# The second mixer's output product in three parts, with projections and taps as filler in its attention

## What is computed

```python
n = rms_norm(h, mix_norm[l])
p = n @ w_in[l]
u_conv, q, k, v, q_mem = jnp.split(p, splits, axis=-1)
y_conv = conv_module(u_conv, ...)            # below
q = apply_rope(rms_norm(q, swa_q_norm[l]), cos, sin)     # 6 heads of 64
k = apply_rope(rms_norm(k, swa_k_norm[l]), cos, sin)     # 2 heads
y_swa = sliding_window_attention(q, k, v, sinks)         # window 128
mkv = rms_norm(mem, mem_norm[l]) @ w_mem_kv[l]           # 256 memory tokens
mk, mv = jnp.split(mkv, 2, axis=-1)
mk, qm = rms_norm(mk, mem_k_norm[l]), rms_norm(q_mem, mem_q_norm[l])
y_mem = memory_attention(qm, mk, mv)                     # 4 heads
y = jnp.concatenate([y_conv, y_swa, y_mem], axis=-1)     # 384 + 384 + 256
h = h + y @ w_out[l]

def conv_module(u, w_dw, b_dw, ln_g, ln_b):
    a, gate = jnp.split(u, 2, axis=-1)                   # 384 channels each
    y = a * jax.nn.sigmoid(gate)
    y = causal_depthwise_conv(y, w_dw, 31 taps) + b_dw
    return jax.nn.silu(layer_norm(y, ln_g, ln_b))
```

## Time and profile before

| | us |
|---|---|
| median of three runs | 2496.94 (2491.99 to 2501.63) |
| the profiled execution | 2497.42 |
| its span | 2495.6 |
| second mixer, first pass, from the last sum of the norm ahead to the last output matmul | 160.3 |
| of it before the first score product / attention / output tiles | 64.6 / 65.9 / 29.8 |
| second mixer, second pass | 164.3 |
| PE busy over the span | 2334.3 |
| VectorE / ScalarE busy over the span | 1543.6 / 1087.3 |

### The profile page before, as it was taken

How to read it: one execution, slowest core, us unless ns; L and a number is a source line. 1 busy time by engine, 2 the same in 40 slices (tenths; PEclk the granted TensorE clock), 3 DMA queues, 4 the chain that set the end, 5 groups by cost and what they waited for, 6 DMA issues and landing times. The chain is left out here.

```text
span 2495.6 us, 37523 instructions
## 1 busy us (share of the span) xinstructions
PE 2334.3 (94%) x13974; PEld 1990.5 (80%) x13974; DVE 1543.6 (62%) x2861; ACT 1087.3 (44%) x1896; POOL 59.4 (2%) x73
## 2 busy tenths in 40 slices
PE   6999989999999999989999999979999999978998
PEld 3656777989976587788998999747997999747997
DVE  4786606677633572376776766763766766763765
ACT  2323334555533234254555554343554554344544
POOL 0000001200000000020000000000000000000000
PEclk8989999999999999999999999979999999979999
DMA  7755222444545423224544554203553455203552
GB/s 310 266 191 188 102 102 78 171 157 181 188 167 221 178 102 127 77 107 174 200 179 154 198 196 177 102 26 139 192 195 131 177 190 188 102 26 125 197 183 92
DMA packets 37540, 390.17 MB, mean 156 GB/s; under 512 B 4416, under 2 KB 5056, under 8 KB 5952
## 3 DMA queue, kind: packets, MB, share of 16 engines
q1 hardware_dynamic: 37440, 388.87, 42.1%
HBM read 387.80 MB, written 1.05 MB: 156 GB/s over the span
## 5 line engine op out<-in xcount | busy, mean ns | idle before, releaser
L1272 PE MATMUL bank<-h,ring 128*128 128x256 f32 x2048 | 476.9, 388 | 9.7 <-ACT h L1063 8.1
L1272 PEld LDWEIGHTS bank<-h,ring 128*128 128x128 f32 x2048 | 388.6, 193 | 100.7 <-issue 29.1
L701 DVE TENSOR_TENSOR ffn_w_lo<-ring,ffn_w_hi 128x2048 fp32r<-128x2048 f32 x126 | 288.8, 2292 | 165.5 <-ACT ffn_w_hi L650 165.4
L571 PE MATMUL bank<-ffn_hh,ffn_w_hi 128*128 128x512 f32 x1408 | 363.9, 399 | 13.3 <-DVE ffn_hh L831 11.0
L571 PEld LDWEIGHTS bank<-ffn_hh,ffn_w_hi 128*128 128x128 f32 x1408 | 257.6, 192 | 67.4 <-issue 10.2
L623 PE MATMUL bank<-ffn_g_hi,ffn_w_hi 128*128 128x256 f32 x1056 | 299.3, 283 | 6.1 <-DVE ffn_g_lo L746 6.1
L623 PE MATMUL bank<-ffn_g_lo,ffn_w_hi 128*128 128x256 f32 x1056 | 298.8, 283 | 0.0
L623 PE MATMUL bank<-ffn_g_hi,ffn_w_lo 128*128 128x256 f32 x1056 | 298.8, 283 | 0.0
L650 ACT ACTIVATE ffn_w_hi<-ring 128x2048 fp32r<-128x2048 f32 x126 | 239.9, 1904 | 0.8
L623 PEld LDWEIGHTS bank<-ffn_g_hi,ffn_w_hi 128*128 128x128 f32 x1056 | 202.7, 192 | 7.4 <-issue 7.4
L623 PEld LDWEIGHTS bank<-ffn_g_hi,ffn_w_lo 128*128 128x128 f32 x1056 | 202.7, 192 | 0.0
(11 more groups left out here) (277 smaller groups left out, 3289.5 us busy)
## 6 DMA issues: line engine op xcount, KB each, us to landing
ring<-w_in SPq DMA_DIRECT2D x244, 1536.0 KB, 6.4
x<-x_in SPq DMA_DIRECT2D x1, 1024.0 KB, 15.2
mem<-mem_in SPq DMA_DIRECT2D x1, 1024.0 KB, 4.9
y_out<-x SPq DMA_DIRECT2D x4, 256.0 KB, 2.5
con<-con_in SPq DMA_DIRECT2D x1, 801.0 KB, 6.9
par<-par_in SPq DMA_DIRECT2D x2, 302.0 KB, 15.6
work<-pos_in SPq DMA_DIRECT2D x2, 128.0 KB, 6.0
par<-par_in SPq DMA_DIRECT2D x2, 76.0 KB, 4.7
```

Source lines behind the costliest of these rows:

```text
L571: pe.matmul(up_out(j, half, False), w_hi[:, j % 2, c0:c0 + P], hh[:, k, :, :], start=k == 0, stop=False)
L701: dve.tensor_tensor(w_lo[:, j % 2, UP], ring[:, (base + j) % RING, UP], w_hi[:, j % 2, UP], ALU.subtract).then_inc(S(tag + "_up_lo"), 1)
L1272: m = pe.matmul(ps[0:m_rows, 0:T], tile(t0 + k, base)[:, 0:m_rows], rhs, start=k == 0, stop=k == len(src) - 1 and kind != "uk")
```

## The change

The list is written out anew, and the parts of it move as follows.

- The memory's norm is split. Its sum on PE (now in bank 6) stands after `q` 1; its Ln, Exp and VectorE's products stand in step 0 of the attention, after `qm` 1 (`("mem", "scale", 0)`).
- The head of the list has `ca` 2, `cg` 2, `cg` 0, `ca` 0, `cg` 1, `k`, `q`, `v`, `qm` 0. `mk` 0 and 1, `ca` 1, `mv` 0 and 1 and six of eight first output parts lie in the attention.
- The taps of a block are summed in two buffers, even taps in `cvo` and odd ones in `cvo_odd`; a tap waits for the last but one, and one add joins the two. The loops over registers are gone. The blocks run one after the other, block 1 in pieces of 6, 6, 6, 6 and 5 taps in steps 4 to 8.
- The output product is made in three parts, `oa` (window attention, three matmuls a tile), `ob` (memory, two) and `oc` (convolution, three). All eight tiles accumulate at once, two to a bank in banks 0 to 3. VectorE adds them to x in pairs after every second `oc`.
- The layer norm uses bank 4, in steps 10 and 11 and after them. The log-and-exp table set is asked for after the last Sigmoid (`cg` 1), the Silu set after the layer norm's Exp.
- The weights are laid out in the new order; their count is the same.

```diff
+IN_ATTENTION = [
+    proj("qm", 1) + [("mem", "scale", 0)],
+    [("sq", "qm", 0)] + proj("mk", 0, 1) + taps(0, 2),
...
+    out_part("oa", 0, 1) + taps(1, 4),
...
+          + out_part("oa", 6, 7) + [("ln", "", 2)] + out_part("ob", *range(8)) + out_part("oc", *range(8)))
+OUT_K = {"oa": (3, 4, 5), "ob": (6, 7), "oc": (0, 1, 2)}
...
-                with dve.Fori(k0, k1) as k:
-                    for i, b_ in enumerate(blocks):
-                        dve.wait_ge(sem, k * n + (i + 1 - n))
-                        dve.scalar_tensor_tensor(cvo[:, b_, :], glu[:, b_, bass.ds(k, T)],
-                                                 par[:, bass.ds(k + (PAR2["conv_w"] + b_ * TAPS), 1)],
-                                                 cvo[:, b_, :], ALU.mult, ALU.add).then_inc(sem, 1)
...
+                dve.tensor_scalar(cvo[:, b_, :], glu[:, b_, 0:T], p2("conv_w", b_ * TAPS), p2("conv_b", b_), ALU.mult,
+                                  ALU.add).then_inc(sem, 1)
+                dve.tensor_scalar(cvo_odd[:, b_, :], glu[:, b_, 1:1 + T], p2("conv_w", b_ * TAPS + 1), None,
+                                  ALU.mult).then_inc(sem, 1)
+
+            def taps_dve(dve, b_, n):
+
+
+                sem, (p0, p1) = S("taps%d" % b_), TAP_PAIRS[b_][n:n + 2]
+                for k in range(2 + 2 * p0, 2 + 2 * p1 + (p1 == 14)):
+                    sums = (cvo_odd if k % 2 else cvo)[:, b_, :]
+                    dve.wait_ge(sem, k - 1)
+                    dve.scalar_tensor_tensor(sums, glu[:, b_, k:k + T], p2("conv_w", b_ * TAPS + k), sums, ALU.mult,
+                                             ALU.add).then_inc(sem, 1)
+                if p1 == 14:
+                    dve.wait_ge(sem, TAPS)
+                    dve.tensor_tensor(cvo[:, b_, :], cvo[:, b_, :], cvo_odd[:, b_, :], ALU.add).then_inc(sem, 1)
...
-                    norm_pe(pe, "mm", bank[2], memh)
                     for step, kind, j in STEPS2:
-                        if step == "proj":
+                        if step == "mem" and kind == "sum":
+                            norm_pe(pe, "mm", bank[6], memh)
...
+                        elif step == "out":
+                            t0, t1 = TILES2[kind, j]
+                            need(pe, seen, base, t0, t1)
+                            if (kind, j) == ("oa", 0):
+                                pe.wait_ge(S("pj_free"), len(pj))
+                                pe.wait_ge(S("ov_free"), 3)
...
+                            if (kind, j) == ("ob", 0):
+                                pe.wait_ge(S("ov_free"), 5)
+                            for n, k in enumerate(OUT_K[kind]):
+                                if (kind, j) == ("oc", 0):
+                                    pe.wait_ge(S("conv_out"), k + 1)
+                                m = pe.matmul(bank[j // 2][:, j % 2 * T:j % 2 * T + T], tile(t0 + n, base), y[:, k, :],
+                                              start=kind == "oa" and j % 2 == 0 and n == 0,
+                                              stop=kind == "oc" and k == 2, skip_group_check=True)
+                            m.then_inc(S("tiles_used"), USED2[kind, j][1])
+                            if kind == "oc" and j % 2 and j >= 3:
+                                next_sum(pe, "o", j - 3)
                                 next_sum(pe, "o", j - 2)
...
-                            if (kind, j) == ("cg", 2):
+                            if (kind, j) == ("cg", 1):
                                 act.preload_act_table_set("natural_log_exp_and_others")
...
+                        elif step == "out" and kind == "oc" and j % 2:
                             dve.wait_ge(S("tiles_used"), USED2[kind, j][0])
-                            dve.tensor_tensor(x[:, j, :], bank[pj[kind, j] % 2][:, 0:T], x[:, j, :],
-                                              ALU.add).then_inc(S("pj_free"), 1)
-                    dve.wait_ge(S("pj_free"), len(pj))
+                            for n in (j - 1, j):
+                                dve.tensor_tensor(x[:, n, :], bank[n // 2][:, n % 2 * T:n % 2 * T + T], x[:, n, :],
+                                                  ALU.add).then_inc(S("x_done"), 1)
+                    dve.wait_ge(S("x_done"), KD)
```

More of the change, by code:

```diff
@@ L241, with norm2, out_part, taps @@
-MIX2 = [(kind, j, 8) for step, kind, j in STEPS2 if step == "proj"]
+TAP_PAIRS = {2: (0, 14), 0: (0, 6, 9, 14), 1: (0, 3, 6, 9, 12, 14)}
+def norm2(key):
+    return [("sum", key, 0), ("rs", key, 0)]
+def out_part(kind, *js):
+    return [("out", kind, j) for j in js]
+def taps(b_, n):
+    return [("taps", "", (b_, n))]
+IN_ATTENTION = [
+    proj("qm", 1) + [("mem", "scale", 0)],
+    [("sq", "qm", 0)] + proj("mk", 0, 1) + taps(0, 2),
+    norm2("qm") + [("sq", "mk", 0)] + proj("ca", 1),
+    norm2("mk"),
+    [("glu", "", 1)] + proj("mv", 0) + taps(1, 0),
+    proj("mv", 1) + taps(1, 1),
+    [("vt", "mv", 0), ("vt", "mv", 1)] + taps(1, 2),
+    taps(1, 3),
+    out_part("oa", 0, 1) + taps(1, 4),
+    out_part("oa", 2, 3),
+    out_part("oa", 4) + [("ln", "", 0)],
+    out_part("oa", 5) + [("ln", "", 1)]]
@@ L244, in ranges @@
+OUT_K = {"oa": (3, 4, 5), "ob": (6, 7), "oc": (0, 1, 2)}
+MIX2 = [(kind, j, len(OUT_K[kind]) if step == "out" else 8) for step, kind, j in STEPS2 if step in ("proj", "out")]
 def ranges(blocks, first_tile):
```

113 lines of the change are left out of this document (49 added, 64 removed).

## The result

The changed kernel takes **2474.4 us** (median of four runs, 2470.2 to 2476.1) against 2497.0 for the kernel before (four runs, 2492.0 to 2501.6). The ratio is 0.9904, with a 95% interval of 0.9887 to 0.9921: 22.7 us or 0.96% faster, beyond the 0.5% that a measurement can tell from nothing. Forecast were 2472, a range of 2459 to 2486, and faster as the likeliest. The profiled execution took 2476.1, its span 2474.3.

What follows compares the result with a forecast made beforehand. The prediction put 36.5 us of a 160.3 us pass down to PE's waits and half clock. Gains of 10.5 us in the first pass and 14.5 in the second, together 25.0, gave 2472 us, range 2459 to 2486.

Steps and rivals of the forecast that it cites:

- The head: Front of the first pass: PE starts its first projection at 1564.6, not 1568.44; half-clock stretch charged again, 1.7 us.
- the walk: Step-by-step timing of the first pass at full clock, 0.1 to 0.2 us a handoff, ending at 1706.5.
- Taps: One block's taps on VectorE, in even and odd sums: 29 cost 11.8 us and not 19.4.
- the sum: First pass at full clock: 1721.44 - 1706.5 - 0.43 = 14.5 us gained, before 4.0 for the clock.
- Table loads: Norms on ScalarE: no load at Ln and Exp, 2.56 us shorter each, 7.7 us in the walk.
- the list of norms: Norms where VectorE's wait for ScalarE was to shorten: first queries, memory queries and memory keys.
- Attention: First pass after the first scores: VectorE sets the middle units, PE is the bound after values end at 1668.0.
- The clock: Half-clock loss in the first pass's attention: 4.0 us taken, between bounds of nothing and 15.4.
- The cover that wasn't: End of the attention: output parts one and two hide the layer norm and its Silu, worth some 6 us.
- The slower rival: Taps on VectorE don't overlap, 0.67 us each: 16.1 us a pass, 7.2 us slower, 2504; chance 0.03.
- More gain: No half clock after the front, or none in the attention: 33 to 38 us, 2459 to 2464; chance 0.10.

Runs made afterwards that it cites:

- e3: The changed kernel with each block's taps in one chain, each waiting for the one before: 2484.4 us, ratio 0.9947 to the kernel before.
- e7: The kernel before, old order, with table sets moved, taps written out and block 2 in even and odd sums: 2487.5 us, ratio 0.9948.
- e2: The changed kernel without its table-set requests, so each norm's Ln and Exp load again: 2493.6 us, ratio 0.9982 to the kernel before.
- e1: The kernel before with only the log-and-exp table set asked for after the last Sigmoid: 2483.5 us, ratio 0.9942 to the kernel before.
- e8: The changed kernel with 13 matmuls nobody reads in PE's waits of the attention: 2465.6 us, ratio 0.9864 to the kernel before.
- e4: The changed kernel with the output product made whole, tile by tile, behind the attention: 2474.8 us, ratio 0.9905 to the kernel before.
- e11: The kernel before, old order, with e1's table sets and 30 matmuls nobody reads in PE's waits: 2468.0 us, ratio 0.9881.
- e5: The changed kernel with the memory's norm whole at the head of the list again: 2465.5 us, ratio 0.9861 to the kernel before.
- e10: Earlier form of e11, with 5, 5, 2 and 2 such matmuls: nine runs between 2472.5 and 2491.0 us, ratio 0.9939 to the kernel before.

## Why the prediction held, point by point

- **The head.** First projection forecast at 1564.6, measured 1564.83; first scores 1614.25 and 1614.19. Right, in the walk and in its parts.
- **Taps.** 29 in 11.8 us forecast, 11.56 measured. Right. What they are worth was never a term of the sum. It is 10 us in the new order (e3), and nothing in the old (e7), where VectorE's faster block ran into a wait for ScalarE.
- **Table loads.** The load between Ln and Exp is gone, and the forecast named 7.7 us a pass; taking the sets out costs 7.6 in the first pass and 9.5 in the second (e2). The size held, the list of norms didn't: it is the memory's norm that gains, not the first queries', where the rope's wait takes it back. That the size came out in spite of this is luck: a norm left out and one too many cost the same. The Trainium skill, "ScalarE: Activation LUTs", section on table sets, says that Ln followed by Exp needs one load. The traces show two where another set was loaded after the joint one had been asked for, and none where it was asked for last; e1 and e2 show that this one line is most of the gain.
- **Attention.** VectorE's wait for the memory's Exp: 4.0 forecast, 4.72 measured. First key projection 1622.8 and 1623.73; the projection ahead of it ran at half clock. Wait ahead of the third turn: 4.0 at 1643.0, measured 3.80 at 1643.67. Right within a microsecond. The wait of 1.6 us forecast ahead of the fourth turn is missing, since the memory-value projection ran partly at the lower clock; with the clock held it is 1.37 (e8).
- **The clock.** Here the step was mis-sized. Forecast were 4.0 us, 1.5 at the first scores and 2.5 at the seventh turn. Against the walk's 1706.5 the last output matmul ended at 1712.8, so 6.3 us are clock and handoffs. Nearly all is the clock: with it held behind 1618.5 (e8) the first pass takes 146.1 us, where the walk has 1706.5 - 1561.1 = 145.4. Taking away the falls of the attention gives 5.5 us in the first pass, against the 2.5 of the forecast, and 3.8 in the second. The fall came one turn earlier than named, ahead of the sixth, and lasted 13.4 us; the first output part started at 1672.47 instead of 1668.0. The pass lengths gained 8.7 and 14.4, where the forecast has 10.9 and 14.9 (10.5 and 14.5 with the 0.43 behind each pass), and 1.8 came back outside the passes, where 0.9 was counted. The first pass is where the forecast missed, and the clock is the term. The second had no walk of its own, only the 4.0 us by which it was longer before; that it met its figure within half a us is luck, since a pass moves by 3 us between two profiled executions.
- **The cover that wasn't.** The prediction said that the parts hide the layer norm and the Silu, "worth some 6 us", and that the output tiles in the attention bring the clock back. Whole output tiles behind the attention take the same time (e4), where this cover would have been some 12 us in two passes. The first output tile doesn't wait for the Silu there either: five of its eight matmuls don't need it, and the layer norm is done in time. The clock came back sooner there. This argument carried no term of the sum, but it would have been wrong as a reason to make the change.
- **The slower rival** was priced with the wrong row. A single chain was taken at 0.67, 16.1 us a pass; written out it costs 0.52, and the whole of it would have made 2484, a smaller gain and not a loss. A row of a chained instruction inside a register loop was not the price of the same instruction written out. By its own terms this rival also decides at 0.62 us a tap and not at 0.61, since 12.5 + 6.5 us are spread over 87 taps.
- **More gain**, 33 to 38 us with no low clock, was about right in size: the 13 added matmuls give 9 to 10 us more, 2465.6, or 31 to 34 in all (e8).

So the time was right for the most part by its terms, and the account of where it comes from was incomplete. Of 22.7 us the table sets are 13 to 19, by the order in which they are taken; the rest goes with the new order and its second chain of taps (e3), more than half of it as less time at half clock (e8, e11), and the order gives up some 10 us by moving the memory's norm (e5). The output parts in the attention have no share in it that these runs can tell (e4).

Open is where a fall of the clock begins and ends. In the first pass of the kernel after it falls at the waits of 3.58, 1.62, 3.80 and 1.51 us and not at the one of 2.43. In the second pass, under the same order, it stays up at the wait of 1.63 us ahead of the first scores, whose projection takes 3.72 us, and falls in the key projections behind the wait of 2.43:

```profile
2170.44 3.72 PE L1869 MATMUL bank<-h,ring 128*128 128x256 f32 x16
...
2177.43 8.83 PE L1869 MATMUL bank<-work,ring 128*128 128x256 f32 x32 [2.43 <-DVE work L542]
```

So the length of a wait does not decide it alone, and the two passes of e10 differ in it under one list.

## What to carry to other kernels

Look at a function table's load before reordering anything: ask for the set with both functions after the last function of another set, since here the position of one request was worth more than the whole rewriting of the order. Before a product is split to serve as filler, find the wait that it would fill; if part of each tile needs none of the late inputs, the whole product behind the stage can hide as much, as it did here. Where PE waits 1 to 4 us and then runs at the lower clock, count that loss, and try a few matmuls that nobody reads in the wait: 13 a pass, 0.43 us each, gave 9 us in a kernel of 2474.

## What the runs showed of the hardware

- A 128x256 fp32 multiply-add on VectorE that waits for the one before costs 0.67 us in a register loop, 0.52 written out (15.07 / 29, e3), and 0.40 where it waits for the one before the last (11.56 / 29). In the loop of the kernel before, with two blocks alternating, it is 0.405 too (7.29 / 18), so the loop made only the single chain dearer. The Trainium skill, "VectorE: DVE Perf Modes", section on the drain, says that leaving out the semaphores between chained operations gains nothing. Between these rows both forms wait on a semaphore, and which operation is waited for makes 0.12 us a tap; whether a chain with no waits would be faster still no run here shows.
- The clock stayed at the lower level for 27 us in which PE had a row open 86% of the time (23.44 of 27.40, e1), and in e4 rose during scores, turns and values, with no 128x256 projection at all. That a projection brings the clock back, as the prediction read from one place, is not what decides.
- Short runs of matmuls in the waits kept the clock up from five us behind the first scores to the end of the output (1.00 over 91.5 us, e8), and 30 of them kept it at 0.99 and 0.98 over the passes of an order that had lost it for 27 us (e11).
